# Page numbers held in registers, a first projection fed piece by piece, and a new order of projections and compressions

## What is computed

```python
q, kvc, kvs, kvw, gates, u, v = _split_proj(_rms(x, norm1_g) @ w_in)      # 544 tokens x 1024 @ 1024 x 2328
past_cmp = cache_cmp[page_table].reshape(Bd, nb, L_BLK, 2, N_KV, HEAD_DIM) # 8 x 16 pages of 128 rows
comp = _compress(past_cmp, pe_cmp, w_cmp1, w_cmp2)                        # gelu(blocks of 64 rows @ w1) @ w2
rows = pool_blocks[phys, :, :, g_ix]                                      # selected pages, keys and values
o_sel = _sel_core(q, t, rows[..., 0, :], rows[..., 1, :], ...)
xs = xs + _mix_out(o_nsa, o_gm, out_norm_g, w_out)
xs = xs + _hier_moe(_rms(xs, norm2_g), ...)                               # 16 SwiGLU experts, 2 per token
```

## Time and profile before

| | us |
|---|---|
| median of 3 runs | 898.24 |
| profiled execution | 896.35 |
| its span | 894.7 |
| TensorE busy | 778.4 (87%) |
| VectorE, ScalarE, GpSimd busy | 233.9, 181.0, 127.8 |
| mean granted TensorE clock | 0.932 |

### The profile page before, as it was taken

One profiled execution on the slowest core, in us unless ns is written; L12 is line 12 of the kernel. 1 busy time (PEld: TensorE's weight loads), 2 busy tenths in 40 slices (PEclk: granted clock), 3 DMA queues, 4 the chain that ended last, 5 costly groups with the idle time before them and its releaser, 6 DMA issues.

```text
span 894.7 us, 14469 instructions
## 1 busy us (share of the span) xinstructions
PE 778.4 (87%) x5320; PEld 564.3 (63%) x5320; DVE 233.9 (26%) x656; ACT 181.0 (20%) x444; POOL 127.8 (14%) x196
## 2 busy tenths in 40 slices
PE   5999969999788736959995699999999999999970
PEld 2574858485445422744554698888888888888840
DVE  4092110473464723451114300000000000000003
ACT  3102130123195422542112000000000000000003
POOL 1203051203300340000001101111111111110010
PEclk9999989999989977989997599999999999999995
DMA  9936261547720572086116257899898989899426
GB/s 354 372 125 195 103 214 55 159 168 236 216 115 2 161 207 103 3 308 266 48 48 246 73 204 267 321 319 323 312 316 316 324 317 321 316 324 325 132 36 224
DMA packets 49992, 189.45 MB, mean 212 GB/s; under 512 B 8145, under 2 KB 25842, under 8 KB 43282
## 3 DMA queue, kind: packets, MB, share of 16 engines
q1 hardware_dynamic: 37090, 152.39, 46.1%
q0 software_dynamic: 12848, 36.36, 14.4%
HBM read 175.32 MB, written 17.33 MB: 215 GB/s over the span
## 4 chain that ended last, share of the span: by engine, by line
PE 80%; issue 4%; DMA 4%; DVE 4%; ACT 3%; POOLq 2%; SPq 2%; POOL 0%; DVEq 0%; ACTq 0%
PE pb L502 74%; POOLq L316 2%; PE pb L957 2%; DMA x_rows<-kvn,qbd 2%; PE pb L742 1%; SPq L316 1%; DMA ring<-in_sel_pages_dram 1%; SPq L319 1%; PE pb L868 1%; DMA xr<-in_xT_dram 1%; DVE xr L1873 1%; PE pb L650 1%; PE pb L903 1%; DMA xr<-x_rows 0%; DMA ugr<-h_rows,qbd 0%
## 5 line engine op out<-in xcount | busy, mean ns | idle before, releaser
L502 PEld LDWEIGHTS pb<-vnr,ring 128*128 128x128 f32 x2048 | 234.0, 194 | 9.6 <-issue 6.7
L502 PE MATMUL pb<-vnr,ring 128*128 128x128 f32 x2048 | 234.4, 277 | 2.3 <-DVE vnr L1823 2.3
L502 PE MATMUL pb<-ring,xr 128*128 128x512 f32 (+3 forms) x640 | 139.4, 415 | 9.7 <-DVE xr L1343 9.7
L502 PEld LDWEIGHTS pb<-ring,xr 128*128 128x128 f32 (+1 forms) x640 | 68.5, 152 | 72.7 <-issue 59.5
L502 PE MATMUL pb<-ring,qT 128*128 128x512 f32 x256 | 112.3, 592 | 0.0
L502 PEld LDWEIGHTS pb<-ring,qT 128*128 128x128 f32 x256 | 47.5, 190 | 54.0 <-issue 54.0
L502 PE MATMUL pb<-ring,work 128*32 128x128 f32 (+2 forms) x512 | 73.6, 389 | 0.0
L1823 DVE COPY vnr<-pb 128x512 f32<-128x512 f32 x16 | 11.1, 692 | 228.2 <-PE pb L957 228.2
L1960 POOL DMA_INDIRECT x_rows<-kvn,qbd x16 | 25.2, 1577 | 300.0 <-DVE kvn L1838 273.6
L502 PE MATMUL pb<-ring 128*128 128x128 f32 (+1 forms) x512 | 62.1, 285 | 6.3 <-issue 6.3
L502 PEld LDWEIGHTS pb<-ring 128*128 128x128 f32 x512 | 61.4, 198 | 6.6 <-issue 6.6
(11 more groups left out here) (301 smaller groups left out, 623.9 us busy)
## 6 DMA issues: line engine op xcount, KB each, us to landing
ring<-in_w_gate_dram SPq DMA_DIRECT2D x16, 2048.0 KB, 9.1
ring<-in_w_up_dram SPq DMA_DIRECT2D x16, 2048.0 KB, 8.9
ring<-in_w_down_dram SPq DMA_DIRECT2D x16, 2048.0 KB, 9.4
ring<-in_cmp_pages_dram SPq DMA_DIRECT2D x64, 128.0 KB, 2.8
ring<-in_cmp_pages_dram POOLq DMA_DIRECT2D x64, 128.0 KB, 3.2
ring<-in_sel_pages_dram SPq DMA_DIRECT2D x64, 128.0 KB, 2.7
ring<-in_sel_pages_dram POOLq DMA_DIRECT2D x64, 128.0 KB, 2.9
ring<-in_w_in_dram SPq DMA_DIRECT2D x3, 2048.0 KB, 9.2
```

Source lines behind the costliest of these rows:

```text
L502: return nc.tensor.matmul(out, lhsT, rhs, start=start, stop=stop)
```

## The change

1. **Page numbers.** `page_numbers` reads all 16 numbers of a set into registers at once, by constant addresses, and `load_pages` only starts transfers. For compression sets 1 to 3 and for half 1 of the selected pages the numbers are read before the wait for the slot.
2. **Keys and values apart.** Half 1 of the selected pages is loaded in two goes of 64 half pages: keys after the last `selected_scores` of half 0 (`sel_mm` 4), values after `samp_pv` 1 and after the keys have landed. `selected_scores(1)` needs keys alone; `sampled_values(1)` waits for the values.
3. **The first projection.** x and the weights of block Q come in five pieces (one, one, two, two, two slices), and TensorE takes a slice for four tiles at a time, in four banks. ScalarE now waits for a piece's weights too.
4. **Loads at the start.** The weights of block KC are asked for before the page table, the constants and `w1`.
5. **Order on TensorE.** Q, KC, compress 0, KW, compress 1, two tiles of V, compress 2, three tiles of V, compress 3, U. The bias product moves from the second KC tile to the second KW tile, and VectorE works the bias out after turning Q and KC. Some banks of PSUM change.

```diff
             return slice(64 * g, 64 * g + 64)
-        def load_pages(eng, first, count, table, dst, name, at_once):
-            def turn(j):
-                held = [eng.value_load(pages[0:1, bass.ds(j + first + k, 1)], min_val=0, max_val=NPOOL - 1)
-                        for k in range(at_once)]
-                for k, page in enumerate(held):
-                    eng.dma_start(dst[:, bass.ds(j * 256 + k * 256, 256)],
-                                  table[bass.ds(page, 1), :, :].rearrange("o p n -> (o p) n")
-                                  ).then_inc(sem(name), 16)
-            if count == at_once:
-                turn(0)
-            else:
-                with eng.Fori(0, count // at_once) as m:
-                    turn(m * at_once)
+        def page_numbers(eng, first):
+            return [eng.value_load(pages[0:1, first + j:first + j + 1], min_val=0, max_val=NPOOL - 1) for j in range(PAGES)]
+        def load_pages(eng, numbers, table, dst, name, part=slice(0, 256)):
+            for j, page in enumerate(numbers):
+                eng.dma_start(dst[:, 256 * j + part.start:256 * j + part.stop],
+                              table[bass.ds(page, 1), :, part].rearrange("o p n -> (o p) n")).then_inc(sem(name), 16)
+        KEYS, VALUES = slice(0, 128), slice(128, 256)
+        PIECES = ((0, 1), (1, 2), (2, 4), (4, 6), (6, 8))
+        PIECE_OF = (0, 1, 2, 2, 3, 3, 4, 4)
         def bank_of(n):
+            if n in (PT, TILES):
+                return pb[7 if n == PT else 4]
             return pb[(0, 1, 4, 5)[n % 4] if n // TILES == BLK_U else n % 4]
+        def turn_bank(t):
+            return pb[5 + t % 2 if t < TILES else 4 + (t + 1) % 2]
         SMALL, STREAM = 3, 2
...
-                load(xr[:, h * TOK:(h + KD // 2) * TOK], t["xT"][:, h * TOK:(h + KD // 2) * TOK], "x_in%d" % (h > 0))
-                load(wv[:, h:h + KD // 2, :], t["w_in"][h * P:(h + KD // 2) * P, a:b].rearrange("(k p) n -> p k n", p=P), "wv_in%d" % (h > 0))
+            for n, (k, end) in enumerate(PIECES):
+                load(xr[:, k * TOK:end * TOK], t["xT"][:, k * TOK:end * TOK], "first_in%d" % n)
+                load(wv[:, k:end, :], t["w_in"][k * P:end * P, a:b].rearrange("(k p) n -> p k n", p=P), "first_in%d" % n)
+            w_in(BLK_KC)
             load(pages[:, :], t["pages"], "pages_in")
             load(cst[:, :], t["consts"], "cst_in")
...
+            load_pages(sp, page_numbers(sp, 0), t["cmp_pages"], cmp_dst, "cmp_in_sp")
             load(lng, t["ln_g"].to_broadcast([P, 512]), "gm_in")
             load(lnb, t["ln_b"].to_broadcast([P, 512]), "gm_in")
             load(tabs[:, 1024:2048], t["ws_t"], "gm_in")
...
-            load_pages(sp, 32, PAGES, t["cmp_pages"], cmp_dst, "cmp_in_sp", 4)
+            load_pages(sp, numbers, t["cmp_pages"], cmp_dst, "cmp_in_sp")
             sp.wait_ge(sem("proj_done"), 2 * TILES)
             w_in(BLK_V)
+            numbers = page_numbers(sp, 64)
             sp.wait_ge(sem("cmp_mm"), 4)
-            load_pages(sp, 64, PAGES, t["cmp_pages"], cmp_dst, "cmp_in_sp", 4)
+            load_pages(sp, numbers, t["cmp_pages"], cmp_dst, "cmp_in_sp")
+            numbers = page_numbers(sp, 96)
             sp.wait_ge(sem("cmp_mm"), 6)
-            load_pages(sp, 96, PAGES, t["cmp_pages"], cmp_dst, "cmp_in_sp", 4)
+            load_pages(sp, numbers, t["cmp_pages"], cmp_dst, "cmp_in_sp")
             sp.wait_ge(sem("proj_done"), 4 * TILES)
             w_in(BLK_U)
...
-            def selected(hf):
+            def selected(hf, part=slice(0, 256), held=None):
                 for q in range(0, HALF, 2):
-                    load_pages(sp, PAGES * (hf * HALF + q), PAGES, t["sel_pages"], ring[:, SEL_SLOT[q], :],
-                               "sel_in%d" % q, 4)
+                    load_pages(sp, held[q] if hf else page_numbers(sp, PAGES * q), t["sel_pages"], ring[:, SEL_SLOT[q], :],
+                               "sel_in%d" % q, part)
             wo = ring[:, 4:6, :].rearrange("p s n -> p (s n)").rearrange("p (k n) -> p k n", k=KD)
@@ -430,15 +438,20 @@
             sp.wait_ge(sem("proj_done"), 5 * TILES)
             state(1)
             for i in range(3):
-                x_rows(i, "x_in0")
+                x_rows(i, "first_in0")
+            held = {q: page_numbers(sp, PAGES * (HALF + q)) for q in (0, 2)}
+            sp.wait_ge(sem("sel_mm"), 4)
+            selected(1, KEYS, held)
             sp.wait_ge(sem("samp_pv"), 1)
-            selected(1)
+            for q in (0, 2):
+                sp.wait_ge(sem("sel_in%d" % q), 16 * 2 * PAGES)
+            selected(1, VALUES, held)
             w_out(0)
             sp.wait_ge(sem("samp_pv"), 2)
             w_out(1)
             sp.wait_ge(sem("attn_done"), 1)
             for i in range(3, TILES):
-                x_rows(i, "x_in1")
+                x_rows(i, "first_in1")
             load(wr, t["w_router"], "router_in")
             load(br, t["b_router"].to_broadcast([P, 20]), "router_in")
             load(g2, t["g2"].to_broadcast([P, D]), "router_in")
...
                     te.wait_ge(sem("w1_in"), 16)
+                    te.wait_ge(sem("proj_out"), TILES)
                 else:
                     te.wait_ge(sem("hc_ready"), 2 * s)
...
                     te.wait_ge(sem("ring_in%d" % WIN_SLOT[nb]), WIN_LOADS[nb])
-                if n >= 4:
+                if n > TILES:
...
             def sampled_values(hf):
                 te.wait_ge(sem("pts_out"), 5 * hf + 5)
+                if hf == 1:
+                    for q in range(HALF):
+                        te.wait_ge(sem("sel_in%d" % q), 16 * 3 * PAGES)
...
-            project(0)
-            project(1)
-            te.wait_ge(sem("ss_ready"), 1)
-            for i in range(PT):
-                mm(pb[6][:, i:i + 1], sq[0][:, P * i:P * i + P], small[:, 0:1])
-            for j in range(4):
-                ins = mm(pb[6][NS * j:NS * j + NS, PT:TILES], sq[0][:, SEQ:TOK], small[:, 0:1])
-            ins.then_inc(sem("rs_mm"), 1)
+            wq = ring[:, WIN_SLOT[BLK_Q], 0:KD * W].rearrange("p (k n) -> p k n", k=KD)
+            for k in range(KD):
+                if k == KD - 2:
+                    te.wait_ge(sem("ss_ready"), 1)
+                    for i in range(PT):
+                        mm(pb[6][:, i:i + 1], sq[0][:, P * i:P * i + P], small[:, 0:1])
+                    for j in range(4):
+                        ins = mm(pb[6][NS * j:NS * j + NS, PT:TILES], sq[0][:, SEQ:TOK], small[:, 0:1])
+                    ins.then_inc(sem("rs_mm"), 1)
+                te.wait_ge(sem("first_in%d" % PIECE_OF[k]), 32)
+                te.wait_ge(sem("xg_ready"), k + 1)
+                for i in range(PT):
+                    ins = mm(pb[i][:, :], xT[:, k, i * P:i * P + P], wq[:, k, :], k == 0, k == KD - 1)
+                    if k == KD - 1:
+                        ins.then_inc(sem("proj_done"), 1)
+            project(PT)
+            project(TILES)
             te.wait_ge(sem("cst_in"), 16)
-            for n in range(2, TILES):
+            turned(0)
+            turned(1)
+            project(TILES + 1)
+            turned(2)
+            turned(3)
+            project(TILES + 2)
+            turned(4)
+            for n in range(TILES + 3, 2 * TILES):
+                turned(n - 3)
                 project(n)
-                turned(n - 2)
-            turned(TILES - 2)
-            turned(TILES - 1)
-            te.wait_ge(sem("rs_ready"), 1)
+            for n in range(2 * TILES - 3, 2 * TILES):
+                turned(n)
             compress(0)
-            for n in range(TILES, 2 * TILES):
-                project(n)
-                if n == TILES + 1:
-                    position_bias()
-                if n > TILES:
-                    turned(n - 1)
-            turned(2 * TILES - 1)
-            compress(1)
             for n in range(2 * TILES, 3 * TILES):
                 project(n)
+                if n == 2 * TILES + 1:
+                    position_bias()
                 if n > 2 * TILES:
                     turned(n - 1)
             turned(3 * TILES - 1)
+            compress(1)
+            for n in range(3 * TILES, 3 * TILES + 2):
+                project(n)
             compress(2)
-            for n in range(3 * TILES, 4 * TILES):
+            for n in range(3 * TILES + 2, 4 * TILES):
                 project(n)
             compress(3)
...
             for k in range(KD):
-                if k % (KD // 2) == 0:
-                    act.wait_ge(sem("x_in%d" % (k > 0)), 16)
+                act.wait_ge(sem("first_in%d" % PIECE_OF[k]), 32)
...
                 V.tensor_scalar(xT[:, k, :], xT[:, k, :], vec[:, k:k + 1], None, ALU.mult).then_inc(sem("xg_ready"), 1)
-            for k in range(1, KD):
-                link(V.tensor_tensor(sq[0], sq[0], sq[k], ALU.add))
+                if k >= 1:
+                    link(V.tensor_tensor(sq[0], sq[0], sq[k], ALU.add))
             dve.sem_inc(sem("ss_ready"), 1)
...
```

(36 more changed lines are left out.)

15 lines of the change are left out of this document (4 added, 11 removed).

## The result

The changed kernel takes 867.3 us (median of 4 runs, 862.9 to 871.2) against 898.3 (897.3 to 898.6): ratio 0.967, 95% interval 0.9635 to 0.9707. The forecast was 866. The profiled execution took 871.22, the slowest of the four; its span is 869.4 at a mean granted clock of 0.94.

A forecast was written before the change was run, and what follows sets the result against it. TensorE, four fifths of the span, was taken as the bound, with time to gain where it waits or clocks low. 3.2 - 1.8 - 0.7 + 8.7 + 23.2 = 32.6 us off 896.35 gave 863.7, median 866, range 861 to 871.

The forecast's parts named there:

- Selected pages: Half 1 of attention: TensorE's 21.49 us wait for the last page and the slow items behind it go, 23.2 us gained.
- Start: Start of the kernel: with smaller first pieces TensorE's first product comes at 6.5 instead of 9.7, 3.2 us gained.
- Turn waits: First projections: four tiles coming out at once make TensorE wait 4.1 us on turns against 1.2 + 1.1 before, 1.8 lost.
- bias: Bias product in KW's stage: VectorE ready 22.7 us after compress 0 begins, TensorE there after 22.1, 0.7 us lost.
- Pages of the compressions: Before compressions 2 to 4: no stall for pages, and no lower clock behind the third's, 8.7 us gained.
- T: Time from freed slot to landed set of compression pages: 24.8 us before, forecast 13.4, bounds 12 and 24.8.
- the pages still gate: Rival at the compressions: T of 18 leaves gaps short by 4.2 and 2.3 us, about 9 us back, 875; chance 0.17.
- The other two signs: Signs of being wrong: half pages land late, or attention shows new waits of several us after the old stall's place.
- The slower rival: Compressions: T stays at 24.8, stalls of 25.2 us plus clock falls of 7.2 eat the whole gain; starving chance 0.03.
- half pages one after another: Rival at half 1's pages: one in flight per queue, keys 46 us late, values 71, some 980; chance 0.01.

The follow-up runs named there:

- registers only: The kernel before with page numbers read into registers, 16 at a time and ahead of the waits, and nothing else: 862.5 and 861.6 us in two series.
- again: The changed kernel run once more, unaltered, with a second profiled execution: median 867.0 us.
- Half the bytes: The changed kernel with sets 1 to 3 of the compressed pages loading 128 of 256 columns: 862.5 us.
- pairs_again: Second series of the kernel before with page numbers in registers, first inputs in five pieces, TensorE taking each slice for two tiles: 863.0 us (859.5 in the first).
- even: The changed kernel with compress 0 after two KC tiles, compress 1 after KC, compress 2 after KW, compress 3 after all of V: 865.0 us.
- old_start: The changed kernel with x and Q's weights in halves, first projection tile by tile, KC's weights behind the first pages: 876.8 us.

## Why the prediction was right, and where it was not

The median was right to 1.3 us, the steps named are the ones that moved, and one term of the sum was mis-sized. Four runs that spread over 8.3 us do not fix a median to 1.3, so that closeness is luck. In the three comparisons the gain is 31.0, 27.7 and 30.9 us, for a forecast of 32.2.

- **Selected pages, 23.2 us.** The stage from the want of keys to the output's turning fell by 23.2 (67.2 to 43.95). But the split into keys and values had no part in it: registers only does the same. With the numbers at hand and whole pages the load is short enough, by 0.2 us in its first trace. The step named one cause for two edits, and only one of them works. The other costs 2.1 us at GpSimd's branch, for which the prediction had no term.
- **Start, 3.2 us.** 9.69 to 6.51.
- **Turn waits, 4.1 us, and bias, 0.7.** 3.4 and 0.45. The places were the ones named.
- **Pages of the compressions, 8.7 us.** This term was mis-sized. The fourth compression ends 7.0 us earlier (8.7 in "again"), where the terms gave 3.2 - 1.8 - 0.7 + 8.7 = 9.4. T was 16.6, not 13.4: the prediction added the old landing of 3.2 us to the issue, a landing measured with a pause after every four pages. It had noted the bytes alone as 10.7 plus the landing, "much the same". With the 0.4 for the signal that is 14.3, already over the gap of 13.8, and it never asked what the landing of the last page in an unbroken burst would be. Half the bytes shows it. This is the rival "the pages still gate" in small: 2.75 + 0.18 us of waiting instead of 6.5, and no fall of the clock right behind it (1.00).
- **A sign of being wrong that came.** "I am wrong if a page set takes over 16 us": the third set took 16.6 in the profiled execution and 15.8 in "again". The other two signs did not come.
- **The slower rival** (the compressions starve if registers save nothing) was a sound mechanism, and its run came out dearer than priced: 32.0 us of waits for 25.2.
- **The profiled execution** was forecast at 863.7 and took 871.22. Of the 7.5 us, 2.4 arose by the fourth compression and 5.5 in the stage behind it, at a granted clock of 0.88 for 0.93; the rest gave 0.7 back. Such a fall comes in some executions and not in others ("again" took 861.93), and the prediction had no term for it. The median was put 1.9 above this execution and lies 3.9 below it.

The prediction also passed over what its own sum said. Start, turns and bias netted 0.7 us, and the page term rested on the registers alone; that the new order put gaps of 13.8 and 15.7 us in place of V's one of 29.5 was counted only as "0.4 above T". Against registers only, "again" gains 3.2 at the first product and ends the fourth compression 1.1 later. The page wait (1.94), the turns (1.1 more than before) and the bias (0.4) account for 3.5 of those 4.3. Another 2.1 of the 4.4 is the step behind GpSimd's branch. The 1.2 that are left lie inside the interval of 1.7 to 7.1. The mean granted clock of the twelve runs is 0.9434, of those of registers only 0.9467, and whether that is more than chance these runs do not show.

In the rival with half pages one after another the prediction used the Trainium skill's figure of 0.95 us for one transfer of 64 KB (DMA: Bandwidth & Descriptors, section Bandwidth). Taken one at a time at that figure, as an estimate, half pages would have been late, by some 4 us for the keys (265.1 + 61 against 321.6) where the prediction wrote 3. They were not taken so: the changed kernel issued all 64 value loads of half 1 within 20 us (290.96 to 310.7), the last landed at 317.2, and nothing waited.

## What to carry to other kernels

Take addresses that are known early into registers before the wait that frees the buffer; a loop that reads and issues in turn held these transfers to half their rate. Then try that edit alone: a reordering made to hide a load has its own waits, and here, once the load was short, the reordering only cost. For a burst without pauses, do not price the last landing by that of transfers issued with pauses; where two estimates of a load stand on either side of the gap that must cover it, take the stall as likely. And compare the chain that ended last to its very end: an edit in the middle of this kernel cost 2.1 us at a branch 550 us later.

## What the runs showed of the hardware

- Two queues that issue 128 KB each every 0.58 us made single landings grow from 2.5 to 7.2 us within one set of 32; with 64 KB each the median was 2.5.
- The step behind a branch on GpSimd took 0.43 us in seven traces and 2.5 to 2.7 in seven others, in which GpSimd's program was longer by the loads of keys and values apart.
- The length of a wait alone does not tell whether the granted clock falls behind it: behind 2.75 us (after) a compression ran at 1.00, behind 0.42 (pairs_again), 0.79 (even) and 2.31 (old_start) one ran at 0.89 and took 1.6 us longer.
- Moving one weight load behind sixteen register reads and sixteen page loads put it 25 us later on SP (issued at 32.8 instead of by 7.4), and the wait it caused (8.95 us) was followed by products at 0.70 of their speed (10.15 for 7.13).
- The spread of this kernel goes with the granted clock: from 872.41 us at 0.935 to 861.93 at 0.950, with the same instructions. Two kernels 3 us apart need a dozen runs each or more, or a comparison place by place in traces in which the same rows took the same time.
